# Where the vector engine norms the spatial gate's values: ahead of the next projection, or inside its first group of tiles

## The chip, the cores and the metric

The kernel runs on one core of one Trainium2 chip, as one program. The metric is device time in microseconds (us). Of the kernel before, three timed runs gave a median of 3325.25 us (3325.23 to 3325.48). Its traced execution took 3323.69 us, of which the trace spans 3322.0 us.

## The reference, cut to what matters

Two models run one after the other on 512 tokens of width 1024. The first has two layers, and only these are touched here. Each layer has a projection with eight parts (q, k, v, g, u, vs, p, gates), three branches (retention, spatial gating, pooling), and a feed-forward block of width 4096. Both halves of a layer are scaled and shifted by `mod`, which comes from the conditioning vector c:

```python
c_act = jax.nn.silu(c)
for l in range(DEPTH):                       # DEPTH = 2
    mod = c_act @ w_ada[l] + b_ada[l]        # 6 x 1024 numbers
    ...
    proj = h @ w_in[l]
    q, k, v, g, u, vs, p, gate_cols = split_columns(proj)
    y_ret = retention(q, k, v, g, positions)
    y_sgu = spatial_gating(u, vs, ws_gmlp[l], bs_gmlp[l], vnorm_gmlp[l])

def spatial_gating(u, v, w_s, b_s, v_gain):
    u = jax.nn.gelu(u)
    v = rms_norm(jax.nn.gelu(v), v_gain)     # over the 1024 channels of a token
    ...
    mixed = jnp.einsum('gts,bnsgc->bntgc', w, vc) + b_s.T[None, None, :, :, None]
    return u * mixed.reshape(B, S, GMLP_WIDTH)
```

The change concerns `v = rms_norm(gelu(v))`: its place among the work of the vector engine.

## The kernel before, in words

**Weights.** All weights come as one stream of 648 tiles of 128x1024 float32 (512 KB each), in the order in which they are used. A tile lands in one of four slots of `raw` (`RING = 4`). The scalar engine (ACT) makes the rounded part `hi[slot]` from it (line 1066), the vector engine (DVE) the rest `lo[slot] = raw - hi` (line 1514), and the tensor engine (PE) forms each product from three matmuls: hi by the high part of the data, hi by its low part, lo by its high part (lines 493 to 495). Both ACT and DVE have a helper `tick(s)` for this; it treats the slot that lies three ahead of the tile being worked on (`AHEAD = 3`). When DVE has made `lo`, it raises `lo_ready`; the sync engine waits for that before it issues the next load into the slot, and PE waits for it before it uses the tile.

**Conditioning sums.** Some of the stream's tiles are not for PE: they hold rows of `w_ada`. In three stages of a layer each group of four weight tiles comes with four such tiles. DVE multiplies one by `c_all` and sums it (`ada_sum`, line 1493) into a column of `four = stat[:, 0:4]`, and this too frees the slot (`lo_ready`). After four of them `take` copies `four` into `mod` (line 1500). The table `ADA_TICKS = ((0, 1), (2, 3, 4), (5, 6), (7,))` says which of the group's eight slots are treated beside tiles 0, 1, 2 and 3: numbers 0 to 3 are conditioning sums, 4 to 7 are weight tiles. ACT goes by the same table, but does nothing for 0 to 3.

**The order around the change.** Each engine runs its own list, in the order in which it is written. The stage before is the projection `vs` (`tiles_N(2, ...)`), token-major, whose four banks ACT drains with a Gelu into `act3` (line 1222). The stage after is the projection `u`, eight tiles (`tiles_T(8, ...)`), called u0 to u7 here, in two groups of four; ACT drains each with a Gelu (line 1216). Of a group, PE needs tile 3 from DVE's number 4 of that same group, and the tiles 0, 1 and 2 of the next group from its numbers 5, 6 and 7. So u4, the first tile of the second group, can begin when DVE has done number 5 of the first group, and the loads for u4 and what follows are issued when slots come free.

**The norm.** Between the two stages DVE waits until ACT has drained the last bank of `vs`, squares and sums each of the four token blocks (line 1822, four times), makes the mean plus epsilon (line 1825) and raises `v_mean`. ACT answers with a square root (line 1255) and raises `rooted`. DVE takes the reciprocal (1829), refines it with one Newton step (1831 to 1835), and scales the four blocks in place (1839). PE waits for the scaled blocks (`v_normed`) only after u7, in front of the mixing matmuls (line 736).

Lines of the loop helper (`repeat`, a hardware loop) show as line 83.

Of the kernel before, what the change touches and what calls it, by code (L numbers as in the profile page):

```python
# [10 lines left out]
ACT = mybir.ActivationFunctionType  # L11
ALU = mybir.AluOpType
# [4 lines left out]
D = 1024  # L17
KT = D // P
TT = S // P
# [5 lines left out]
EPS = 1e-6  # L25
# [67 lines left out]
def build(nc, stream, first, xT, cvec, pos, consts, decay, tables, vec1, ws, bs, vec2, wf, outT):  # L93
    with ExitStack() as ctx:
# [18 lines left out]
        yF = sb("yF", [P, 2 * KT * S])  # L113
        with nc.sbuf_tensor("halved", [P, 3 * KT, S], F32R) as halved:
            pass
        act3 = sb("act3", [P, 3 * KT, S])
# [18 lines left out]
        stat = sb("stat", [P, 16])  # L135
# [124 lines left out]
        bank_free = sem("bank_free")  # L260
# [24 lines left out]
        rooted = sem("rooted")  # L285
# [11 lines left out]
        v_mean = sem("v_mean")  # L297
        v_normed = sem("v_normed")
# [750 lines left out]
        def _(act):  # L1049
# [58 lines left out]
            def tiles_N(groups, drain, ada=False):  # L1108
                def body(i):
                    for s in range(2 * RING if ada else RING):  # L1110
                        tick(s, ada=ada and s < RING)
                    for t in range(TT):
                        token_wait(t)
                        drain(i, t)
                bodies(groups, {tok: 3, **(ada_ring if ada else {})}, body)
# [95 lines left out]
            for l in range(LAYERS):  # L1211
                round_h(mod[:, 0:8], tick_at=2)

                def drain_to(first, func):
                    def drain(i, s):
                        act.activation(act3[:, at(i * RING + s + first), :], pb[:, s:s + 1], func  # L1216
                                       ).then_inc(bank_free, 1)
                    return drain

                def drain_tok(first, func):  # L1220
                    def drain(i, t):
                        act.activation(act3[:, bass.ds(i + first + 2 * t, 1), :], pb[:, t:t + 1], func
                                       ).then_inc(bank_free, 1)
                    return drain
                tiles_T(8, lambda i, s: None, uses_st=False, peel=True)
                tiles_N(2, drain_tok(8, ACT.Copy))

                def head_out(h):

                    for e in range(2):  # L1230
                        o = pb[:, 2 + 2 * (h % 2) + e]
                        act.wait_ge(o_full, of.next())
                        act.activation(A[:, h + 4 * e], o, ACT.Copy)
                        act.activation(Osq[h % 2][:, e * S:(e + 1) * S], o, ACT.Square).then_inc(osq_ready, 1)

                def root_of(h):

                    act.wait_ge(summed, sums.next())
                    act.activation(stat[:, 8:12], pb[:, 0 if h < 2 else 6, 0:4], ACT.Sqrt, bias=epsc,
                                   scale=1.0 / R_V).then_inc(rooted, 1)  # L1240

                act.activation(cs[:, 2, 0:1], epsc, ACT.Sqrt)
                head_out(0)
                head_out(1)
                root_of(0)
                head_out(2)
                root_of(1)
                head_out(3)
                root_of(2)
                root_of(3)  # L1250
                tiles_T(8, lambda i, s: to_st(s, func=ACT.Silu))
                pairs(True)
                tiles_N(2, drain_tok(8, ACT.Gelu_apprx_tanh), ada=True)
                act.wait_ge(v_mean, means.next())
                act.activation(stat[:, 8:12], stat[:, 12:16], ACT.Sqrt).then_inc(rooted, 1)
                tiles_T(8, drain_to(0, ACT.Gelu_apprx_tanh), uses_st=False, ada=True)

                for n in range(KT):
                    s = n % RING
                    tick(s)  # L1260
                    act.wait_ge(tile_done, done.next())
                    act.wait_ge(y_ready, l * 56 + (8 + n + 1))
                    act.activation(A[:, n], pb[:, s], ACT.Copy).then_inc(bank_free, 1)
                pairs()
                for g in range(4):
                    tick(g)
                    act.wait_ge(tile_done, done.next())
                    for e in range(2):
                        n = 2 * g + e

                        to_st(n % 4, scale=v1[:, span(l * V_ALL + (V_PS + n), 1)], bias=bpps[:, n:n + 1])
                pairs(True)
                tick(0)
                to_x(peel=True)
                root()
                round_h(mod[:, 24:32])
                tiles_T(8, lambda i, s: to_st(s), peel=True)
                with repeat(act, 3, {split: 16, done: 16, stf: 8, **{c: 64 for c in land}}):
                    tiles_T(8, lambda i, s: None, uses_st=False)
                    tiles_T(8, lambda i, s: to_st(s))  # L1280
                if l < LAYERS - 1:
                    to_x()
                    root(then_tick=False)
                else:
                    act.wait_ge(gain_ready, 1)
                    late_tiles(to_late(hH, gain2, double=True))
# [179 lines left out]
            work = to_late(yH, v2[:, W_FFN + 8:W_FFN + 16])  # L1466
# [13 lines left out]
        def _(dve):  # L1480
            split, drained = Count(), Count(4)
# [15 lines left out]
            def take(i, m):  # L1497

                dve.drain()
                dve.tensor_copy(mod[:, bass.ds(i * RING + m, RING)], four)  # L1500
                dve.drain()
# [22 lines left out]
                    with repeat(dve, n, steps or ring) as i:  # L1524
                        body(i)

            def tiles_T(n, work, last=False, peel=False, ada=None, from_bank=False):
                def body(i, first=False):
                    for s in range(RING):
                        t = None if not last else TILES - RING * (n // RING - i) + s  # L1530
                        if ada is not None:
                            for j in ADA_TICKS[s]:
                                tick(j, ada=four[:, j:j + 1] if j < RING else None)
                            if s == 1:
                                take(i, ada)
                        elif s or not first:
                            tick(s, t)
                        done.next()
                        if work is None:
                            drained.next()  # L1540
                        elif from_bank:
                            drained.next()
                            dve.wait_ge(tile_done, done.value())
                            work(i, s)
                        else:
                            dve.wait_ge(bank_free, drained.next())
                            work(i, s)
                if peel:
                    body(0, True)
                    bodies(n // RING - 1, lambda i: body(i + 1))  # L1550
                    return
                bodies(n // RING, body, last, {**ring, **lands(2)} if ada is not None else None)
# [18 lines left out]
            roots = Count()  # L1571
# [177 lines left out]
            for l in range(LAYERS):  # L1749
# [66 lines left out]
                pairs(True, ada=16)  # L1816
                tiles_N(2, ada=32)

                dve.wait_ge(bank_free, drained.value())
                for t in range(TT):  # L1820
                    vt = act3[:, 8 + 2 * t:10 + 2 * t].rearrange("p a s -> p (a s)")
                    dve.tensor_tensor_reduce(yF[:, 0:1024], vt, vt, 1.0, 0.0, ALU.mult, ALU.add,
                                             stat[:, 8 + t:9 + t])
                    dve.drain()
                dve.tensor_scalar(stat[:, 12:16], stat[:, 8:12], 1.0 / D, EPS, ALU.mult, ALU.add)
                dve.drain().then_inc(v_mean, 1)
                y, v, t = stat[:, 8:12], stat[:, 12:16], stat[:, 4:8]
                dve.wait_ge(rooted, roots.next())
                dve.reciprocal(y, y)
                dve.drain()  # L1830
                dve.scalar_tensor_tensor(t, y, -0.5, y, ALU.mult, ALU.mult)
                dve.drain()
                dve.tensor_tensor(t, t, v, ALU.mult)
                dve.drain()
                dve.scalar_tensor_tensor(y, t, 1.5, y, ALU.add, ALU.mult)
                dve.drain()
                for t in range(TT):
                    vt = act3[:, 8 + 2 * t:10 + 2 * t].rearrange("p a s -> p (a s)")
                    dve.tensor_scalar(vt, vt, stat[:, 8 + t:9 + t], None, ALU.mult).then_inc(v_normed, 1)
                tiles_T(8, None, ada=40)  # L1840
                add_bias(l, 16, 48)
                dve.wait_ge(bank_free, drained.value())
                for n in range(KT):
# [473 lines left out]
```

## Time and profile before

| what | value |
|---|---|
| median of three timed runs | 3325.25 us (3325.23 to 3325.48) |
| profiled execution: own time | 3323.69 us |
| profiled execution: span of the trace | 3322.0 us |
| PE busy | 3273.8 us, 99% of the span |
| PE weight load busy (overlaps PE) | 2697.3 us, 81% |
| DVE busy | 1877.9 us, 57% |
| ACT busy | 1144.0 us, 34% |
| POOL busy | 146.6 us, 4% |
| chain that ended last | PE 90%, DVE 5%, the rest under 2% each |
| mean rate of the loads | 108 GB/s |

The own time includes 1.69 us that lie outside the trace's span. "Busy" counts the engine's instructions; a matmul of 512 columns shows as 0.39 us, though the next one starts 0.23 us later, since they overlap. In part 5 of the page a group's row ends in: busy us, mean ns of one | idle us before them, what ended most of it. So the pace of PE is read from the starts of its matmuls, not from their durations. A number in brackets behind a row is the time that the engine sat idle before it, and what ended that.

### The profile page before, as it was taken

The page shows a single profiled execution, that of the slowest core. Times are in us where ns is not written, and L with a number is a line of the kernel's source. Part 1 is how long each engine was busy: PE and PEld are TensorE (multiplying, and loading weights), DVE is VectorE, ACT ScalarE, POOL GpSimd, SP SyncE. Part 2 cuts the span into 40 slices and gives each one's busy share as a digit, 9 for nine tenths or more (in the row PEclk, how much of TensorE's full clock was granted, in tenths as well). Part 3 has the DMA queues.
Part 4 walks back from the last instruction along what each step waited for, and adds up shares of the span by engine and source line. Part 5 has one row for each costly group of instructions (what it writes and reads, how often), then busy time and mean ns, then how long its engine had stood idle before and what let it go on. Part 6 is the DMA issues. An engine that isn't in the chain of part 4 may idle for free.

```text
span 3322.0 us, 43128 instructions
## 1 busy us (share of the span) xinstructions
PE 3273.8 (99%) x15164; PEld 2697.3 (81%) x15164; DVE 1877.9 (57%) x2695; ACT 1144.0 (34%) x1494; POOL 146.6 (4%) x174
## 2 busy tenths in 40 slices
PE   7999999999999999999999999999999999999998
PEld 6788887888888788887888888768888887888887
DVE  6355557554446355557554445556665744576655
ACT  3333333332222233333332223364333513443333
POOL 1000000000000000000000002021000101010000
PEclk9999999999999999999999999999999999999999
DMA  6136424422222145324422222202222222112222
GB/s 232 70 127 210 145 89 146 158 89 95 95 101 83 64 142 200 140 88 160 150 89 95 95 101 87 83 20 89 102 101 96 102 102 83 45 69 101 97 95 76
DMA packets 98232, 357.79 MB, mean 108 GB/s; under 512 B 11104, under 2 KB 11120, under 8 KB 97856
## 3 DMA queue, kind: packets, MB, share of 16 engines
q1 hardware_dynamic: 97344, 353.73, 29.9%
q0 software_dynamic: 768, 2.47, 0.2%
q8 instruction: 75, 1.23, 0.1%
q14 instruction: 45, 0.37, 0.0%
HBM read 354.06 MB, written 2.10 MB: 107 GB/s over the span
## 4 chain that ended last, share of the span: by engine, by line
PE 90%; DVE 5%; issue 1%; ACT 1%; DMA 1%; DVEq 1%; SPq 0%; POOLq 0%; POOL 0%; ACTq 0%
PE pb L493 22%; PE pb L494 22%; PE pb L495 22%; PE pb L523 3%; PE pb L524 3%; PE pb L527 3%; PE pb L561 2%; PE pb L563 2%; PE pb L562 2%; DVE lo L1514 1%; PE pb L893 1%; PE pb L675 1%; DMA raw<-stream 1%; PE pb L998 1%; PE pb L847 1%
## 5 line engine op out<-in xcount | busy, mean ns | idle before, releaser
L1066 ACT ACTIVATE hi<-raw 128x1024 fp32r<-128x1024 f32 x549 | 577.4, 1056 | 995.6 <-PE pb L495 655.3
L1514 DVE TENSOR_TENSOR lo<-raw,hi 128x1024 fp32r<-128x1024 f32 (+1 forms) x549 | 671.6, 1228 | 369.8 <-ACT hi L1066 323.8
L493 PE MATMUL pb<-yH,hi 128*128 128x512 f32 x1648 | 641.6, 389 | 2.5 <-DVE lo L1514 2.5
L494 PE MATMUL pb<-yL,hi 128*128 128x512 f32 x1648 | 641.1, 389 | 0.0
L495 PE MATMUL pb<-yH,lo 128*128 128x512 f32 x1648 | 641.1, 389 | 0.0
L493 PE MATMUL pb<-hH,hi 128*128 128x512 f32 x1528 | 597.1, 391 | 4.3 <-DVE lo L1514 4.3
L495 PE MATMUL pb<-hH,lo 128*128 128x512 f32 x1528 | 594.6, 389 | 0.0
L494 PE MATMUL pb<-hL,hi 128*128 128x512 f32 x1528 | 594.6, 389 | 0.0
L493 PEld LDWEIGHTS pb<-yH,hi 128*128 128x128 f32 x1648 | 309.4, 188 | 67.7 <-ACT st L1079 3.3
L495 PEld LDWEIGHTS pb<-yH,lo 128*128 128x128 f32 x1648 | 309.4, 188 | 64.4
L494 PEld LDWEIGHTS pb<-yL,hi 128*128 128x128 f32 x1648 | 309.3, 188 | 64.0
L493 PEld LDWEIGHTS pb<-hH,hi 128*128 128x128 f32 x1528 | 286.9, 188 | 65.0 <-ACT act L1216 3.1
L495 PEld LDWEIGHTS pb<-hH,lo 128*128 128x128 f32 x1528 | 286.8, 188 | 59.8
L494 PEld LDWEIGHTS pb<-hL,hi 128*128 128x128 f32 x1528 | 287.0, 188 | 58.4
L1079 ACT ACTIVATE st<-pb 128x512 f32<-128x512 f32 x176 | 105.5, 599 | 508.9 <-PE pb L495 495.9
L1662 DVE SCALAR_TENSOR_TENSOR x<-pb,mod,x 128x512 f32 (+1 forms) x72 | 54.1, 751 | 192.8 <-PE pb L495 171.6
L493 PE MATMUL pb<-halved,hi 128*128 128x512 f32 x364 | 142.1, 390 | 2.2 <-DVE lo L1514 1.3
L495 PE MATMUL pb<-halved,lo 128*128 128x512 f32 x364 | 141.6, 389 | 0.0
L494 PE MATMUL pb<-halved,hi 128*128 128x512 f32 x364 | 141.6, 389 | 0.0
L1493 DVE CUSTOM_DVE_ANT_0 raw<-raw,pb 128x1024 f32<-128x1024 f32 x96 | 112.5, 1218 | 39.0 <-ACT st L1079 24.1
L1956 DVE TENSOR_TENSOR st<-pb,tab 128x512 f32<-128x512 f32 x88 | 60.9, 692 | 89.8 <-PE pb L495 66.8
L402 POOL TENSOR_TENSOR act<-act 128x512 f32<-128x512 f32 x25 | 33.8, 1352 | 1699.6 <-ACT act L1120 1699.0
(341 smaller groups left out, 3873.4 us busy)
## 6 DMA issues: line engine op xcount, KB each, us to landing
raw<-stream SPq DMA_DIRECT2D x648, 512.0 KB, 3.2
yF<-first SPq DMA_DIRECT2D x8, 512.0 KB, 12.9
act<-first SPq DMA_DIRECT2D x8, 512.0 KB, 17.5
x<-xT SPq DMA_DIRECT2D x1, 2048.0 KB, 9.3
outT<-act SPq DMA_DIRECT2D x8, 256.0 KB, 2.2
tab<-decay SPq DMA_DIRECT2D x1, 1024.0 KB, 6.5
scr<-ws POOLq DMA_DIRECT2D x2, 256.0 KB, 4.3
scr<-bs POOLq DMA_DIRECT2D x2, 256.0 KB, 5.4
```

The source lines that it names most:

```text
L493: pe.matmul(out, whi, ahi, start=first, stop=False)
L494: pe.matmul(out, whi, alo, start=False, stop=False)
L495: return pe.matmul(out, wlo, ahi, start=False, stop=last)
L523: pe.matmul(pb[:, s], hi[:, s, w], aH[:, k], start=k == 0, stop=False)
L524: pe.matmul(pb[:, s], lo[:, s, w], aH[:, k], start=False, stop=False)
L527: ins = pe.matmul(pb[:, s], hi[:, s, w], aL[:, k], start=False, stop=k == ks - 1)
L561: pe.matmul(pb[:, t], aH[:, k, a], hi[:, s, w], start=k == 0, stop=False)
L562: pe.matmul(pb[:, t], aL[:, k, a], hi[:, s, w], start=False, stop=False)
L1066: act.activation(hi[:, s], raw[:, s], ACT.Copy).then_inc(hi_ready, 1)
L1079: act.activation(st[:, s:s + 1], pb[:, b:b + 1], func, bias=bias, scale=scale).then_inc(bank_free, 1)
L1493: dve.tensor_tensor_reduce(w, w, c_all, 1.0, 0.0, ALU.mult, ALU.add, m).then_inc(lo_ready, 1)
L1514: dve.tensor_tensor(lo[:, s, 0:width], raw[:, s, 0:width], hi[:, s, 0:width].bitcast(F32), ALU.subtract).then_inc(lo_ready, 1)
```

## The change

DVE no longer does the norm ahead of the stage `u`, but within its first group of four tiles: behind conditioning sums 0 to 3, the weight tile number 4 and `take`, ahead of the weight tiles 5, 6 and 7. For this the call of eight tiles becomes two calls of four on DVE and on ACT, and DVE's `tiles_T` gets an argument `between` with a function that runs in the group's second step. On ACT the square root moves from ahead of the eight drains to between the first four and the last four. The wait for the drained banks of `vs` goes with the norm. PE, POOL and the sync engine keep their lists.

```diff
@@ ACT
                 tiles_N(2, drain_tok(8, ACT.Gelu_apprx_tanh), ada=True)
+                tiles_T(4, drain_to(0, ACT.Gelu_apprx_tanh), uses_st=False, ada=True)
                 act.wait_ge(v_mean, means.next())
                 act.activation(stat[:, 8:12], stat[:, 12:16], ACT.Sqrt).then_inc(rooted, 1)
-                tiles_T(8, drain_to(0, ACT.Gelu_apprx_tanh), uses_st=False, ada=True)
+                tiles_T(4, drain_to(4, ACT.Gelu_apprx_tanh), uses_st=False, ada=True)
@@ DVE, the helper
-            def tiles_T(n, work, last=False, peel=False, ada=None, from_bank=False):
+            def tiles_T(n, work, last=False, peel=False, ada=None, from_bank=False, between={}):
 ...
                             if s == 1:
                                 take(i, ada)
+                            if s in between:
+                                between[s]()
@@ DVE, the stage
                 tiles_N(2, ada=32)
 
-                dve.wait_ge(bank_free, drained.value())
-                for t in range(TT):
+                def v_norm():
+
+                    for t in range(TT):
 ...
-                tiles_T(8, None, ada=40)
+                v_drained = drained.value()
+                tiles_T(4, None, ada=40, between={1: lambda: (dve.wait_ge(bank_free, v_drained), v_norm())})
+                tiles_T(4, None, ada=44)
```

The body of `v_norm` is the norm's code as it was, from the sums of squares to the scaling.

DVE's list of instructions from the end of the stage `vs` on, before. `yF` takes the squares, `stat` the small statistics, `act` are the values of `vs`, and `lo<-raw,hi` is a weight tile of line 1514:

```order
L1500 COPY mod<-stat 128x4
...
L1822 ISA yF,stat<-act 128x1024 [waits bank_free]
...
L1829 RECIPROCAL stat<-stat 128x4 [waits rooted]
...
L1839 TENSOR_SCALAR act<-act,stat 128x1024 x4
...
L1493 ISA raw,stat<-raw,pb 128x1024 [waits landed3]
...
L1514 TENSOR_TENSOR lo<-raw,hi 128x1024 [waits hi_ready]
```

The same stretch of DVE's list with the change (its lines stand one to seven further down in the file):

```order
L1501 COPY mod<-stat 128x4
...
L1494 ISA raw,stat<-raw,pb 128x1024 [waits landed3]
...
L1515 TENSOR_TENSOR lo<-raw,hi 128x1024 [waits hi_ready]
L1501 COPY mod<-stat 128x4
L1826 ISA yF,stat<-act 128x1024 [waits bank_free]
...
L1833 RECIPROCAL stat<-stat 128x4 [waits rooted]
...
L1843 TENSOR_SCALAR act<-act,stat 128x1024 x4
L1515 TENSOR_TENSOR lo<-raw,hi 128x1024 [waits hi_ready] x3
```

The four sums and the first weight tile have moved ahead of the norm; the three other weight tiles of the group stand behind it, and so behind its wait for `rooted`.

ACT's list at the same place, before. `stat<-stat` is the square root, `act<-pb` drains a tile of `u`, `hi<-raw` is the rounded part of a weight tile:

```order
L1255 ACT_TABLE_LOAD
L1255 ACTIVATE stat<-stat 128x4 [waits v_mean]
...
L1216 ISA [waits tile_done]
L1216 ACT_TABLE_LOAD
L1216 ACTIVATE act<-pb 128x512
...
L1066 ACTIVATE hi<-raw 128x1024 [waits tile_done]
```

And with the change:

```order
L1216 ACTIVATE act<-pb 128x512 [waits tile_done]
L1066 ACTIVATE hi<-raw 128x1024 [waits tile_done,landed3]
L1216 ACTIVATE act<-pb 128x512 [waits tile_done]
L1066 ACTIVATE hi<-raw 128x1024 [waits tile_done,landed0]
L1066 ACTIVATE hi<-raw 128x1024 [waits tile_done,landed1]
L1216 ACTIVATE act<-pb 128x512 [waits tile_done]
L1066 ACTIVATE hi<-raw 128x1024 [waits tile_done,landed2]
L1216 ACTIVATE act<-pb 128x512 [waits tile_done]
...
L1256 ACT_TABLE_LOAD
L1256 ACTIVATE stat<-stat 128x4 [waits v_mean]
```

The square root has moved behind the drains of u0, u1, u2 and u3, each of which waits until PE has finished that tile.

## Rows read from the trace of the kernel before

**Rows 1.** Page, parts 4 and 5: chain by engine; the costliest ACT group.
```profile
PE 90%; DVE 5%; issue 1%; ACT 1%; DMA 1%; DVEq 1%; SPq 0%; POOLq 0%; POOL 0%; ACTq 0%
L1066 ACT ACTIVATE hi<-raw 128x1024 fp32r<-128x1024 f32 x549 | 577.4, 1056 | 995.6 <-PE pb L495 655.3
```

**Rows 2.** Waits of PE: who was waited for, total us, times, longest us.
```profile
PE pb L493 <- DVE lo L1514: 8.1, 8, 1.3
```

**Rows 3.** Timeline of PE, first layer: start us, us, instruction [idle before].
```profile
344.24 0.39 PE L493 MATMUL pb<-hH,hi 128*128 128x512 f32 x1
...
360.33 0.39 PE L495 MATMUL pb<-hH,lo 128*128 128x512 f32 x1
361.76 0.49 PE L493 MATMUL pb<-hH,hi 128*128 128x512 f32 x1 [1.05 <-DVE lo L1514]
...
367.10 0.39 PE L495 MATMUL pb<-hH,lo 128*128 128x512 f32 x1
367.33 0.39 PE L493 MATMUL pb<-hH,hi 128*128 128x512 f32 x1
```

**Rows 4.** Timeline of PE, second layer, the same place.
```profile
1352.26 0.39 PE L495 MATMUL pb<-hH,lo 128*128 128x512 f32 x1
1353.90 0.49 PE L493 MATMUL pb<-hH,hi 128*128 128x512 f32 x1 [1.25 <-DVE lo L1514]
...
1359.45 0.39 PE L493 MATMUL pb<-hH,hi 128*128 128x512 f32 x1
```

**Rows 5.** Timeline of DVE, first layer, around the norm.
```profile
345.17 1.22 DVE L1822 CUSTOM_DVE_ANT_0 yF<-act 128x1024 f32<-128x1024 f32 x1 [3.49 <-ACT act L1222]
...
350.99 0.18 DVE L1829 RECIPROCAL stat<-stat 128x4 f32<-128x4 f32 x1 [0.30 <-ACT stat L1255]
...
351.95 2.74 DVE L1839 TENSOR_SCALAR act<-act,stat 128x1024 f32<-128x1024 f32 x4
354.61 1.22 DVE L1493 CUSTOM_DVE_ANT_0 raw<-raw,pb 128x1024 f32<-128x1024 f32 x1
...
360.41 1.23 DVE L1514 TENSOR_TENSOR lo<-raw,hi 128x1024 fp32r<-128x1024 f32 x1 [1.15 <-ACT hi L1066]
```

**Rows 6.** Timeline of ACT, first layer, around the square root.
```profile
344.53 0.60 ACT L1222 ACTIVATE act<-pb 128x512 f32 x1 [0.76 <-PE pb L563]
345.15 1.28 ACT L1255 ACT_TABLE_LOAD   x1
350.75 0.21 ACT L1255 ACTIVATE stat<-stat 128x4 f32<-128x4 f32 x1 [4.31 <-DVEq L1826]
350.98 1.28 ACT L1216 ACT_TABLE_LOAD   x1
352.28 0.60 ACT L1216 ACTIVATE act<-pb 128x512 f32 x1
...
367.63 0.60 ACT L1216 ACTIVATE act<-pb 128x512 f32 x1 [1.86 <-PE pb L495]
```

**Rows 7.** The line that issues the loads, 340 to 390 us: landing.
```profile
DMA to landing us min/median/max: 3.1/4.3/5.3
```

**Rows 8.** Timeline of PE after idle times of 3.91 and 2.52 us.
```profile
43.73 0.79 PE L523 MATMUL pb<-hH,hi 128*128 128x512 f32 x1 [3.91 <-ACT hH L1183]
...
45.18 0.63 PE L524 MATMUL pb<-hH,lo 128*128 128x512 f32 x1
45.61 0.63 PE L523 MATMUL pb<-hH,hi 128*128 128x512 f32 x1
...
47.59 0.39 PE L523 MATMUL pb<-hH,hi 128*128 128x512 f32 x1
...
2947.17 0.47 PE L523 MATMUL pb<-yH,hi 128*128 128x512 f32 x1 [2.52 <-DVE x L2173]
2947.47 0.40 PE L524 MATMUL pb<-yH,lo 128*128 128x512 f32 x1
```

**Rows 9.** Windows: us, busy of PE, PEld, DVE, ACT, POOL, PEclk, DMA share, GB/s.
```profile
2030.50:2033.90 3.40, 3.40 (x10) 2.60 (x9) 1.08 (x7) 0.00 (x0) 0.00 (x0) 0.51 0.03 7
```

More of the change, by code:

```diff
@@ L1817, in _ @@
                 tiles_N(2, ada=32)
-                dve.wait_ge(bank_free, drained.value())
-                for t in range(TT):
-                    vt = act3[:, 8 + 2 * t:10 + 2 * t].rearrange("p a s -> p (a s)")
-                    dve.tensor_tensor_reduce(yF[:, 0:1024], vt, vt, 1.0, 0.0, ALU.mult, ALU.add,
-                                             stat[:, 8 + t:9 + t])
-                    dve.drain()
-                dve.tensor_scalar(stat[:, 12:16], stat[:, 8:12], 1.0 / D, EPS, ALU.mult, ALU.add)
@@ L1826, in _ @@
[L1826 to L1839, printed above, removed]
-                tiles_T(8, None, ada=40)
+                def v_norm():
+                    for t in range(TT):
+                        vt = act3[:, 8 + 2 * t:10 + 2 * t].rearrange("p a s -> p (a s)")
+                        dve.tensor_tensor_reduce(yF[:, 0:1024], vt, vt, 1.0, 0.0, ALU.mult, ALU.add,
+                                                 stat[:, 8 + t:9 + t])
+                        dve.drain()
+                    dve.tensor_scalar(stat[:, 12:16], stat[:, 8:12], 1.0 / D, EPS, ALU.mult, ALU.add)
+                    dve.drain().then_inc(v_mean, 1)
+                    y, v, t = stat[:, 8:12], stat[:, 12:16], stat[:, 4:8]
+                    dve.wait_ge(rooted, roots.next())
+                    dve.reciprocal(y, y)
+                    dve.drain()
+                    dve.scalar_tensor_tensor(t, y, -0.5, y, ALU.mult, ALU.mult)
+                    dve.drain()
+                    dve.tensor_tensor(t, t, v, ALU.mult)
+                    dve.drain()
+                    dve.scalar_tensor_tensor(y, t, 1.5, y, ALU.add, ALU.mult)
+                    dve.drain()
+                    for t in range(TT):
+                        vt = act3[:, 8 + 2 * t:10 + 2 * t].rearrange("p a s -> p (a s)")
+                        dve.tensor_scalar(vt, vt, stat[:, 8 + t:9 + t], None, ALU.mult).then_inc(v_normed, 1)
```

## The prediction

> **What bounds the kernel.** I read the page first, then the waits of PE, then the timelines of PE, DVE and ACT about the place of the change, in both layers. The chain that ended last is PE for 90% and DVE for 5% [rows 1]: a change on DVE or ACT counts only by the time for which it makes PE wait. The waits of PE hold one kind that fits here: PE's weight tile not ready, because DVE had not made its `lo` part, eight times, 8.1 us in all [rows 2]. The timeline of PE shows two of these at the changed place. In the first layer 72 matmuls (u0, u1, u2) run from 344.24 at 0.2266 us each (71 steps up to 360.33), so u3 could begin at 360.56; it begins at 361.76 [rows 3]. That is 1.20 us lost. In the second layer it is 1353.90 against 1352.49, so 1.41 us [rows 4]. The reason is in DVE's timeline: it waits 3.49 us for the last drain of `vs`, norms from 345.17 to 354.61, and only then frees slots by its sums, so u3's weights land late and their `lo` starts at 360.41 [rows 5].
>
> So the most that this place can give back is 1.20 + 1.41 = 2.6 us, 0.08% of the run.
>
> **What the change does, step by step.** No arithmetic is added or taken away: what moves is the norm of one layer's values (four squares with sums, the mean, the Newton step, four scalings on DVE; the square root and its table load on ACT), once in each of the two layers. The two engines' lists of the first four tiles decide the rest.
>
> *The sums and u3's weights.* DVE had nothing to do for the 3.49 us ahead of 345.17 [rows 5], so its four sums (1.22 us each) start near 341.7 and free slots some 13 us earlier than before (354.61). A load lands at most 5.3 us after its issue [rows 7]. The rounded part of u3's weights stands on ACT behind the drain of u0. u0's last matmul starts at 344.24 + 23 x 0.2266 = 349.45; a drain starts 0.53 us after the last matmul of its tile (367.10 to 367.63) [rows 3, 6], so at 349.98, takes 0.60, and `hi` takes 1.06 [rows 1]. `lo` is made by about 352.9, and PE wants u3 at 360.56. The old stall goes, with more than 7 us to spare.
>
> *The norm up to its mean.* It begins near 353.4, and takes what it took, 5.5 us from 345.17 up to the reciprocal's wait (350.69) [rows 5]. `v_mean` is up at about 359. An error of several us here changes nothing, as the next step shows.
>
> *The square root.* This is the step that decides. On ACT it now stands behind the drains of u0 to u3, and the last of them waits for PE to finish u3. DVE meanwhile stands at the reciprocal, which waits for `rooted`, and behind this on DVE stand weight tiles 5, 6 and 7 of the group, the first of which is u4's `lo`. PE can't begin u4 without it. So PE finishes u3, and only then starts a chain that it has to wait for in full:
> - u3 begins at 360.56 (no stall now), its last matmul at 360.56 + 5.21 = 365.77, PE is out of work at 366.00;
> - ACT drains u3 from 366.30 (0.53 later, as above);
> - the load of the root's table starts 0.62 later (344.53 to 345.15), at 366.92 [rows 6];
> - the root starts 1.30 after its table load, by the pair 350.98 and 352.28 [rows 6], at 368.22;
> - the reciprocal starts 0.24 after the root (350.75 to 350.99) [rows 5, 6], at 368.46;
> - reciprocal and Newton step take 0.96 up to 351.95, the four scalings 2.66 more up to 354.61 [rows 5]: 372.08;
> - `lo` of u4 starts there, and PE starts 1.35 after a `lo` started (360.41 to 361.76) [rows 3, 5]: 373.43.
>
> PE idles from 366.00 to 373.43, 7.4 us. Before, u4 began at 367.33 [rows 3]: 6.10 us lost in the first layer. In the second layer u0 began at 1352.49 - 16.32 = 1336.17, so u4 will begin 29.19 later, at 1365.36, against 1359.45 [rows 4]: 5.91 us. Together 12.0 us. The 2.6 us of the old stalls are already counted in this as gained.
>
> The Trainium skill ("ScalarE: Activation LUTs", What ACT_TABLE_LOAD costs) puts a switch of tables at about 2.66 us, a load of 1.28 and a drain behind it. The trace has 1.28 for the load and 1.30 from its start to the next activation [rows 6], so here nothing shows behind it. By the page each chain would be 1.36 us longer.
>
> *The clock of PE.* An idle time as long as 7.4 us is nowhere in the stretches shown, so it is bounded from both sides. After 3.91 us idle (at the start of the program) the matmuls came at 0.43 us a step from 43.73 to 47.59, instead of 0.23: nine matmuls in 3.86 us which else take 2.04, so 1.8 us lost [rows 8]. In a stretch near 2030 us the granted clock was 0.51 for 3.4 us, which is the level of 1.2 GHz and costs 1.7 us [rows 9]. After 2.52 us idle the pace was full, 1.2 GHz did not show [rows 8]: 0 us. An idle time of 7.4 us is past the longer of the two, so I take 1.8 us a layer, and 3.6 for both. The lower end is 0; the upper is a low clock twice as long as seen, 3.6 a layer, 7.2 for both. A gain from idling is excluded, since the pace is full before. The Trainium skill ("TensorE: Matmul & The Clock Gate", Why this matters for your kernels) also has idle gaps between matmul bursts bring the low clock back; the row after 3.91 us agrees.
>
> *What comes behind.* The second group starts on DVE with its `lo` tiles at 372.1 and 1.23 us each, then its sums: the first sum is done near 377, and it issues the load of u7's weights, landed by 382.3 at the latest [rows 7]. The last of the four sums waits for the slot freed near 375.8, landed by 381.1. `hi` and `lo` of u7 are done by about 385.5; PE wants u7 at 373.43 + 3 x 5.44 = 389.8. So no second stall, with 4 us of cover. `v_normed` is up at 372.1, and PE asks for it behind u7, over 20 us later. The loads of the mixing stage are later by less than PE is. All of the rest shifts as a whole, and nothing there waits for a fixed time, so nothing is given back.
>
> **The sum.** 6.1 + 5.9 + 3.6 = 15.6 us. On the profiled execution's own time that is 3323.69 + 15.6 = 3339.3. The median of the runs is 1.56 above this execution, so for the median 3325.25 + 15.6 = 3340.9 us, slower by 0.47%.
>
> **Rivals.**
>
> *The stall without the low clock.* For it: the 2.52 us idle that left no trace. Against it: 3.91 us that did. It gives 3325.25 + 12.0 = 3337.3. 10%.
>
> *No stall at all, so not slower.* The place is the wait for `rooted`. PE is not held if the reciprocal starts by 366.00 - 1.35 - 2.66 - 0.96 = 361.03. The mean is up at 359, so this holds if ACT takes the square root between two drains, at 361 or before. Then the chain hides, the old stalls go, and the time is 3325.25 - 2.6 = 3322.6, within the bound of 0.2%. Against it: each engine runs its list in order, and in ACT's list the root stands behind u3's drain, which can't start before 366.30. 3%.
>
> *The change has no effect worth seeing.* Stall out, stall in, of about the same size: it needs the chain behind u3 to be some 6 us shorter than its pieces, that is a step missing, such as the table load and the four scalings (1.30 and 2.66) off the path. Nothing in the lists lets them off. About 3325, 2%.
>
> *The table switch costs what the page says.* The root never followed its table load directly in the trace (345.15, then 350.75 [rows 6]), so the pair that I used belongs to the Gelu. If the root waits longer behind the load, by as much as the load itself again (1.28), each layer loses 1.3 more: 3343.5. 4%. By the page's own 1.36 it would be 3343.6.
>
> *The second group starves too.* The cover of 4 us is used up only if a load lands 9 us after its issue, against 5.3 at most. Each us beyond costs 1 us a layer; with one, 3342.9. 3%.
>
> **Chances and range.** The forecast holds the remaining 78%, with a range of its own of 3338.5 to 3344.5 (clock costs 1 to 7.2 us, half a us either way on the chains). For 8 in 10 with room for the case without the low clock: 3336.5 to 3345.0. A difference under 0.2% (6.7 us) is about what a measurement of this kernel can't tell from no change. Faster by over that: 1%, since even the best case gives 2.6 us. Within it: 5%, the two cases without a net stall. Slower: 94%.
>
> **What would show it.** In PE's timeline of the changed kernel, no idle time ahead of u3, and about 7.4 us idle ahead of the matmul that begins u4, once in each layer, released by DVE's `lo`. On DVE about 9 us idle ahead of the reciprocal, released by ACT's square root. On ACT the root about 2 us behind the drain of u3's bank. Matmuls at 0.43 us a step for 3 to 4 us from u4's start, and a granted clock under 1 there. Sums of the first group from near 342. I am wrong if the reciprocal starts before ACT drained u3, if PE idles under 5 us, or if the second group shows idle time of PE again.

## The result and the profile after

The changed kernel took 3340.69 us (median of six runs, 3338.76 to 3341.45), the kernel before 3325.24 us beside it (six runs, 3322.98 to 3327.50). The ratio is 1.0047, with a 95% interval of 1.0037 to 1.0058: slower by 0.47%. The forecast was 3340.9 us, with a range of 3336.5 to 3345.0. In a second session the changed kernel took 3340.35 us against 3325.04, ratio 1.0046 (1.0032 to 1.0060).

The profiled execution after took 3341.19 us with a span of 3339.5, against 3323.69 and 3322.0: 17.5 us more.

Page of the changed kernel, part 4 (chain by engine) and the first row of its waits of PE (us in total, times, longest us), which answer to [rows 1, 2]:

```profile
PE 91%; DVE 4%; issue 1%; DMA 1%; ACT 1%; DVEq 1%; SPq 0%; POOLq 0%; POOL 0%; ACTq 0%
```

```profile
PE pb L493 <- DVE lo L1515: 19.9, 8, 7.2
```

Eight waits as before, but 19.9 us in place of 8.1, and the longest 7.2 in place of 1.3. Timeline of PE, first layer, against [rows 3]:

```profile
344.94 0.39 PE L493 MATMUL pb<-hH,hi 128*128 128x512 f32 x1
...
361.25 0.39 PE L493 MATMUL pb<-hH,hi 128*128 128x512 f32 x1
...
366.47 0.39 PE L495 MATMUL pb<-hH,lo 128*128 128x512 f32 x1
374.02 0.79 PE L493 MATMUL pb<-hH,hi 128*128 128x512 f32 x1 [7.16 <-DVE lo L1515]
374.60 0.63 PE L494 MATMUL pb<-hL,hi 128*128 128x512 f32 x1
375.03 0.63 PE L495 MATMUL pb<-hH,lo 128*128 128x512 f32 x1
...
379.30 0.63 PE L493 MATMUL pb<-hH,hi 128*128 128x512 f32 x1
379.72 0.53 PE L494 MATMUL pb<-hL,hi 128*128 128x512 f32 x1
380.09 0.40 PE L495 MATMUL pb<-hH,lo 128*128 128x512 f32 x1
```

u0 begins at 344.94, 0.70 us later than before for reasons that lie ahead of the change. u3 begins at 361.25, 72 steps of 0.2266 behind it: the old idle time is gone. PE is out of work at 366.70 and begins u4 at 374.02, 7.3 us later; then it steps at 0.43 us until 380. The second layer, against [rows 4]:

```profile
1366.02 0.39 PE L495 MATMUL pb<-hH,lo 128*128 128x512 f32 x1
1373.57 0.79 PE L493 MATMUL pb<-hH,hi 128*128 128x512 f32 x1 [7.17 <-DVE lo L1515]
...
1376.30 0.58 PE L493 MATMUL pb<-hH,hi 128*128 128x512 f32 x1
1376.71 0.40 PE L494 MATMUL pb<-hL,hi 128*128 128x512 f32 x1
```

Timeline of DVE in the changed kernel, first layer, against [rows 5]:

```profile
342.72 1.22 DVE L1494 CUSTOM_DVE_ANT_0 raw<-raw,pb 128x1024 f32<-128x1024 f32 x1 [0.35 <-issue]
...
352.15 1.23 DVE L1515 TENSOR_TENSOR lo<-raw,hi 128x1024 fp32r<-128x1024 f32 x1 [4.78 <-ACT hi L1066]
353.47 0.17 DVE L1501 COPY mod<-stat 128x4 f32<-128x4 f32 x1
353.76 1.23 DVE L1826 CUSTOM_DVE_ANT_0 yF<-act 128x1024 f32<-128x1024 f32 x1
...
359.11 0.17 DVE L1829 TENSOR_SCALAR stat<-stat 128x4 f32<-128x4 f32 x1
369.04 0.18 DVE L1833 RECIPROCAL stat<-stat 128x4 f32<-128x4 f32 x1 [9.76 <-ACT stat L1256]
...
370.01 2.74 DVE L1843 TENSOR_SCALAR act<-act,stat 128x1024 f32<-128x1024 f32 x4
372.66 3.49 DVE L1515 TENSOR_TENSOR lo<-raw,hi 128x1024 fp32r<-128x1024 f32 x3
```

The mean is done at 359.28, and DVE then stands still for 9.76 us. Timeline of ACT, against [rows 6]:

```profile
361.45 0.60 ACT L1216 ACTIVATE act<-pb 128x512 f32<-128x512 f32 x1 [2.95 <-PE pb L495]
...
366.89 0.60 ACT L1216 ACTIVATE act<-pb 128x512 f32<-128x512 f32 x1 [3.89 <-PE pb L495]
367.51 1.28 ACT L1256 ACT_TABLE_LOAD   x1
368.80 0.21 ACT L1256 ACTIVATE stat<-stat 128x4 f32<-128x4 f32 x1
```

u3's drain at 366.89, the table load behind it, the root at 368.80, the reciprocal at 369.04: the chain of the prediction. ACT itself was idle for 3.89 us ahead of that drain, with the mean long there; it stood in its list at a drain whose tile PE had not finished.

Windows of the changed kernel (us, busy of PE, PEld, DVE, ACT, POOL, PEclk, DMA share, GB/s), against [rows 9]:

```profile
369.40:373.40 4.00, 0.00 (x0) 0.00 (x0) 3.77 (x8) 0.91 (x1) 0.00 (x0) 0.54 0.00 0
373.40:377.00 3.60, 2.98 (x7) 2.41 (x8) 3.60 (x4) 0.00 (x0) 0.00 (x0) 0.50 0.44 162
```

The granted clock falls to its lower level, 1.2 GHz, while PE still waits, and is there when u4 begins.

### The profile page after: what moved, and what is told of

It is laid out like the page before. It is cut to its first block, busy times and chain, and to the rows that moved or that the text cites. A ratio compares the mean times of both kernels' runs of the same rounds, so it can differ in the third digit from the quotient of the medians.

```text
span 3339.5 us, 43062 instructions
## 1 busy us (share of the span) xinstructions
PE 3279.7 (98%) x15164; PEld 2701.8 (81%) x15164; DVE 1878.0 (56%) x2695; ACT 1141.5 (34%) x1492; POOL 146.6 (4%) x174
## 4 chain that ended last, share of the span: by engine, by line
PE 91%; DVE 4%; issue 1%; DMA 1%; ACT 1%; DVEq 1%; SPq 0%; POOLq 0%; POOL 0%; ACTq 0%
PE pb L493 23%; PE pb L494 23%; PE pb L495 23%; PE pb L523 3%; PE pb L524 3%; PE pb L527 3%; PE pb L561 2%; PE pb L562 2%; PE pb L563 2%; DVE lo L1515 1%; PE pb L893 1%; PE pb L675 1%; DMA raw<-stream 1%; PE pb L985 1%; PE pb L998 1%
## 5 line engine op out<-in xcount | busy, mean ns | idle before, releaser
L493 PE MATMUL pb<-hH,hi 128*128 128x512 f32 x1528 | 599.1, 392 | 16.3 <-DVE lo L1515 16.3
```

The source lines that it names most:

```text
L493: pe.matmul(out, whi, ahi, start=first, stop=False)
```

## The experiments

All are timed against the kernel before beside them, and each stands as edits of the changed kernel unless said otherwise.

### The root somewhere else on ACT

`e1_root_before_u2`: the square root and its wait go behind the `hi` parts of tiles 5 and 6.

```diff
+                            if s in between:
+                                between[s]()
...
-                tiles_T(4, drain_to(0, ACT.Gelu_apprx_tanh), uses_st=False, ada=True)
-                act.wait_ge(v_mean, means.next())
-                act.activation(stat[:, 8:12], stat[:, 12:16], ACT.Sqrt).then_inc(rooted, 1)
+                def v_root():
+
+                    act.wait_ge(v_mean, means.next())
+                    act.activation(stat[:, 8:12], stat[:, 12:16], ACT.Sqrt).then_inc(rooted, 1)
+
+                tiles_T(4, drain_to(0, ACT.Gelu_apprx_tanh), uses_st=False, ada=True, between={2: v_root})
```

(The first two lines stand in ACT's `tiles_T`, behind the weight tiles of step `s`.)

> The changed kernel, but ACT takes the square root behind the hi parts of tiles 5 and 6 and ahead of its wait for u2, in place of behind u3's drain. DVE's list is that of the changed kernel. Theory (the root stands behind u3's drain, DVE waits there, and u4's lo stands behind the wait): in the changed kernel the mean is up at 359.3 and ACT is free from 358.5, so the root comes near 360, the reciprocal right after, u4's lo near 364, some 2 us before PE wants it. No idle time of PE ahead of u3 or u4, no low clock: 2.6 us under the kernel before, near 3322.6 (ratio 0.999). Rival (DVE's order alone costs, the norm in the group is simply too much work there): PE idles several us ahead of u4, 3330 or more. Rival (the extra switch of ACT's tables between drains holds the hi parts or the banks): an idle time of some 1 to 3 us later in the group.

Measured: 3321.33 us (11 runs) against 3325.10, ratio 0.9990 (0.9981 to 0.9999). PE's waits for `lo` are six in all, and none stands in this stage. Timelines of ACT and DVE of this kernel, first layer:

```profile
357.90 1.28 ACT L1259 ACT_TABLE_LOAD   x1
359.20 0.20 ACT L1259 ACTIVATE stat<-stat 128x4 f32<-128x4 f32 x1
359.42 1.28 ACT L1218 ACT_TABLE_LOAD   x1
360.83 0.60 ACT L1218 ACTIVATE act<-pb 128x512 f32<-128x512 f32 x1
```

```profile
359.43 0.18 DVE L1838 RECIPROCAL stat<-stat 128x4 f32<-128x4 f32 x1 [0.78 <-ACT stat L1259]
...
363.06 3.49 DVE L1520 TENSOR_TENSOR lo<-raw,hi 128x1024 fp32r<-128x1024 f32 x3
```

DVE waits 0.78 us for the root in place of 9.76, and u4's `lo` starts at 363.06, in time. DVE's list is the same as in the changed kernel. So the place of one instruction on ACT carries the whole loss: 3340.7 against 3321.3. The rival that DVE's order alone costs is out, and so is the one of the added table switch.

### The norm somewhere else on DVE

`e3_norm_between_groups`: ACT's list is that of the changed kernel; on DVE the norm goes behind tiles 5, 6 and 7.

```diff
-                tiles_T(4, None, ada=40, between={1: lambda: (dve.wait_ge(bank_free, v_drained), v_norm())})
+                tiles_T(4, None, ada=40)
+                dve.wait_ge(bank_free, v_drained)
+                v_norm()
                 tiles_T(4, None, ada=44)
```

> The changed kernel, but DVE does the whole norm between the two groups of four tiles, behind weight tiles 5, 6 and 7 of the first. ACT's list is that of the changed kernel, so the root still stands behind u3's drain, and DVE still waits for it. Theory (what costs is that u4's lo stands behind that wait, not the wait itself): DVE waits as long, up to about 368.4 us, but PE has u4, u5 and u6 ready. u7's weights are freed late, near 373, lo by about 380, PE wants them at 382. No idle time of PE: near 3322.6 (ratio 0.999). Rival (DVE's 9 us of waiting cost in any place): 3337 or more. Rival (u7 now comes late): an idle time of up to 3 us ahead of u7, about 3325 to 3330.

Measured: 3322.33 us (11 runs), ratio 0.9991 (0.9982 to 1.0000). No idle time of PE in this stage. But one part of the expectation missed. Timeline of DVE:

```profile
361.88 1.23 DVE L1515 TENSOR_TENSOR lo<-raw,hi 128x1024 fp32r<-128x1024 f32 x1 [3.08 <-ACT hi L1066]
363.02 1.22 DVE L1826 CUSTOM_DVE_ANT_0 yF<-act 128x1024 f32<-128x1024 f32 x1
...
368.83 0.18 DVE L1833 RECIPROCAL stat<-stat 128x4 f32<-128x4 f32 x1 [0.30 <-ACT stat L1256]
```

I had DVE wait long for the root here too. It does not: tile 7's `hi` comes at 361.88 only, so the squares start at 363.02 and the mean is later than u3's drain; ACT waits for DVE. What the run shows is still the point: the root comes even later than in the changed kernel, 3.1 us behind the end of u3 (368.59 and 365.54) against 2.1, and with u4's `lo` ahead of the wait for it, PE loses nothing. That a wait of 9 us on DVE would cost nothing in this place is not shown, since here DVE waits for 0.30 us only.

`e7_norm_before_tile4`: only the four sums go ahead of the norm, and the root is where it was before, ahead of all drains.

```diff
-                tiles_T(4, drain_to(0, ACT.Gelu_apprx_tanh), uses_st=False, ada=True)
                 act.wait_ge(v_mean, means.next())
                 act.activation(stat[:, 8:12], stat[:, 12:16], ACT.Sqrt).then_inc(rooted, 1)
+                tiles_T(4, drain_to(0, ACT.Gelu_apprx_tanh), uses_st=False, ada=True)
...
-                tiles_T(4, None, ada=40, between={1: lambda: (dve.wait_ge(bank_free, v_drained), v_norm())})
+                tiles_T(4, None, ada=40, between={4: lambda: (dve.wait_ge(bank_free, v_drained), v_norm())})
```

(`between` is asked here with the number of the tile, ahead of its `tick`.)

> DVE does the four conditioning sums first, then the norm, then weight tiles 4 to 7; ACT takes the square root ahead of all drains of u, as in the kernel before. This moves the sums alone ahead of the norm. Theory (the sums free the slots; the root is the only other thing that matters): norm from 347 to about 356.5, u3's lo near 358, 2.6 us before PE wants it at 360.6; no idle time ahead of u3 or u4: near 3322.6 (ratio 0.999). Rival (the old idle time ahead of u3 came from ACT, which drains u0 late because of the root): u3 still 1 us late, 3325.

Measured: 3322.49 us (11 runs), ratio 0.9993 (0.9984 to 1.0002), which alone can't be told from no change. The trace can: u3's `lo` starts at 355.87 and no idle time of PE is left at u3 or u4. So the old idle time came from the sums standing behind the norm, and not from ACT, where the root still stands ahead of all drains.

`e2_split_only`: the kernel before, with its call of eight tiles cut in two on both engines.

```diff
-                tiles_T(8, drain_to(0, ACT.Gelu_apprx_tanh), uses_st=False, ada=True)
+                tiles_T(4, drain_to(0, ACT.Gelu_apprx_tanh), uses_st=False, ada=True)
+                tiles_T(4, drain_to(4, ACT.Gelu_apprx_tanh), uses_st=False, ada=True)
...
-                tiles_T(8, None, ada=40)
+                tiles_T(4, None, ada=40)
+                tiles_T(4, None, ada=44)
```

> The kernel before, with the call of eight tiles cut into two calls of four on DVE and ACT, and the norm and the root where they were. Theory: cutting costs nothing, 3325.2 and the old idle times of 1.2 and 1.4 us ahead of u3 stay (ratio 1.000). Rival (loop entry and exit, or other code, costs time on ACT or DVE): idle time of PE ahead of u4 too, some tenths to 2 us a layer.

Measured: 3325.03 us (11 runs), ratio 1.0002 (0.9993 to 1.0011). The old waits stand where they stood (timeline of PE, both layers), and there are no others in the stage:

```profile
361.62 0.49 PE L493 MATMUL pb<-hH,hi 128*128 128x512 f32 x1 [1.08 <-DVE lo L1515]
...
1353.81 0.49 PE L493 MATMUL pb<-hH,hi 128*128 128x512 f32 x1 [1.24 <-DVE lo L1515]
```

### The sizes of the terms

`e5_scale_late`: the four scalings leave the chain.

```diff
+                def v_scale():
+
                     for t in range(TT):
                         vt = act3[:, 8 + 2 * t:10 + 2 * t].rearrange("p a s -> p (a s)")
                         dve.tensor_scalar(vt, vt, stat[:, 8 + t:9 + t], None, ALU.mult).then_inc(v_normed, 1)
...
                 tiles_T(4, None, ada=40, between={1: lambda: (dve.wait_ge(bank_free, v_drained), v_norm())})
+                v_scale()
                 tiles_T(4, None, ada=44)
```

> The changed kernel, but the four scalings of the norm stand between the two groups of tiles, behind weight tiles 5, 6 and 7; squares, mean, root and Newton step stay inside the first group. Theory (every step between u3's drain and u4's lo is on the path at its full length): u4 begins 2.66 us earlier in each layer, PE idles 4.7 us in place of 7.3. The low clock may stay (4.7 us is past the 3.9 after which it was seen): 3340.7 - 5.3 = 3335.4, less if the low clock gets shorter, down to 3331.5 if it goes. Rival (other work hides behind the scalings): less than 2 us gained in all.

Measured: 3335.16 us (6 runs), ratio 1.0032 (1.0020 to 1.0044). Timeline of PE, first layer:

```profile
365.65 0.39 PE L495 MATMUL pb<-hH,lo 128*128 128x512 f32 x1
370.56 0.79 PE L493 MATMUL pb<-hH,hi 128*128 128x512 f32 x1 [4.52 <-DVE lo L1515]
```

From the end of u3 (365.88) to u4 it is 4.68 us, 2.64 less than the 7.32 of the changed kernel: the scalings (2.65 from 370.01 to 372.66 there) were on the path at their full length.

`e6_no_gelu_u`: a root of a constant ahead of the drains loads the table; the drains of u are copies, so the Gelu of u is left out.

```diff
+                act.activation(cs[:, 2, 0:1], epsc, ACT.Sqrt)
-                tiles_T(4, drain_to(0, ACT.Gelu_apprx_tanh), uses_st=False, ada=True)
+                tiles_T(4, drain_to(0, ACT.Copy), uses_st=False, ada=True)
                 act.wait_ge(v_mean, means.next())
                 act.activation(stat[:, 8:12], stat[:, 12:16], ACT.Sqrt).then_inc(rooted, 1)
-                tiles_T(4, drain_to(4, ACT.Gelu_apprx_tanh), uses_st=False, ada=True)
+                tiles_T(4, drain_to(4, ACT.Copy), uses_st=False, ada=True)
```

> The changed kernel, with the eight tiles of u drained by a plain copy; the Gelu of u is left out. So ACT can load the root's table ahead of the drains, and the root follows u3's drain without a load. Theory (the table load of 1.28 us is on the path): PE idles 6.0 us in place of 7.3 ahead of u4, 2.6 us less in all, 3338 with the low clock as it was. Rival (a page of the notes has 1.38 us more behind each switch of tables): 2.7 us a layer less, 3335. Rival (the load is hidden): no difference, 3340.7.

Measured: 3337.97 us (5 runs), ratio 1.0040 (1.0026 to 1.0054). Timelines of ACT and of PE, first layer:

```profile
366.37 0.60 ACT L1216 ACTIVATE act<-pb 128x512 f32<-128x512 f32 x1 [3.89 <-PE pb L495]
366.87 0.20 ACT L1257 ACTIVATE stat<-stat 128x4 f32<-128x4 f32 x1
```

```profile
365.95 0.39 PE L495 MATMUL pb<-hH,lo 128*128 128x512 f32 x1
372.08 0.79 PE L493 MATMUL pb<-hH,hi 128*128 128x512 f32 x1 [5.74 <-DVE lo L1516]
```

From the drain's start to the root it is 0.50 us, against 1.91 in the changed kernel, and PE waits 5.90 us, 1.42 less. So the table load was on the path, and it costs what the trace shows of it, 1.3 us, with a tenth more. The larger price of the Trainium skill ("ScalarE: Activation LUTs", What ACT_TABLE_LOAD costs), 2.66 us for a switch, would have taken 1.2 us more off each wait; this run does not bear it out.

`e4_busy_pe`: PE is kept at work between u3 and u4.

```diff
-                tiles_T(8, hH, hL, None, ada=True)
+                tiles_T(4, hH, hL, None, ada=True)
+                for _ in range(30):
+                    pe.matmul(pb[:, 5], hH[:, 0, 0:P], hH[:, 0], start=True, stop=True)
+                tiles_T(4, hH, hL, None, ada=True)
```

> The changed kernel, with 30 matmuls of 512 columns into an unused bank between u3 and u4 on PE (their product is used by nothing), 6.8 us at full pace, so that PE works through its 7.3 us of waiting. Theory (behind the wait PE runs at 1.2 GHz for a while, and this is 2.8 us in the first layer and 1.3 in the second of the trace of the changed kernel): no matmul at 0.43 us a step behind u4's start, u4 begins when it did, and the time falls by about 4 us against the changed kernel, to 3337. Rival (the low clock costs nothing that counts, since DVE and the loads would set the pace of the second group anyway): the time stays at 3340.7.

Measured: 3337.52 us (5 runs), ratio 1.0038 (1.0024 to 1.0051), beside 3340.35 for `after_again`. Timeline of PE, first layer, and windows (columns as above):

```profile
365.45 6.96 PE L729 MATMUL pb<-hH 128*128 128x512 f32 x30
372.70 0.50 PE L493 MATMUL pb<-hH,hi 128*128 128x512 f32 x1 [0.29 <-DVE lo L1518]
373.04 0.40 PE L494 MATMUL pb<-hL,hi 128*128 128x512 f32 x1
373.27 0.39 PE L495 MATMUL pb<-hH,lo 128*128 128x512 f32 x1
```

```profile
365.50:372.50 7.00, 6.91 (x31) 5.39 (x29) 4.40 (x9) 3.37 (x4) 0.00 (x0) 1.00 0.00 0
372.50:378.00 5.50, 5.30 (x23) 4.42 (x24) 4.77 (x7) 0.00 (x0) 0.00 (x0) 1.00 0.67 210
```

u4 begins 7.25 us behind the end of u3, as late as in the changed kernel, but at 0.23 us a step. The medians differ by 2.8 us where 4 were expected; with runs that spread over 3 us that is no contradiction. The slowest of the five runs (3338.24) is under the fastest of `after_again` (3338.65), so the low clock costs time.

`after_again`, the changed kernel beside these:

> The changed kernel once more, beside the others on one chip. Theory: 15 us over the kernel before, 3340.7, with a spread of 1 to 3 us between runs as the low clock behind each wait comes out shorter or longer.

Measured: 3340.35 us (5 runs, 3338.65 to 3341.71).

## Why the prediction was right

**The bound.** PE sets the time, and DVE and ACT count only through its waits. All runs agree: each median is that of the kernel before plus what PE's timeline shows in this stage, waits and low clock, to within 1.2 us (`e1_root_before_u2` is furthest off: 3.8 us gained where the two idle times hold 2.6).

**The sums and u3.** Right: sums from 342.72, the norm from 353.76 (forecast: near 353.4, on a program that starts 0.7 us earlier), no wait ahead of u3. `e7_norm_before_tile4` shows that this part alone takes both old idle times away, the 2.6 us.

**The chain behind u3.** Forecast 7.43 us from the end of u3 to u4, measured 7.32 in both layers; the difference is the drain of u3, which starts 0.42 us after the last matmul (366.47 to 366.89) and not 0.53. Counted from u0's start, u4 begins at 29.08 in place of 29.19. Before, it was 23.09 and 23.28 (1359.45 - 1336.17), so the loss is 5.99 and 5.80 us, 11.8 in all against 12.0. The experiments took two links out, and each gave back its length: 2.64 for the scalings, 1.42 for the table load.

**The low clock.** The mechanism was right, the size somewhat low. In the first layer 14 steps took 6.07 us (374.02 to 380.09) which at full pace take 3.17, so 2.9 lost; in the second, seven steps took 3.14 (1373.57 to 1376.71) for 1.59, so 1.6 lost. Together 4.5 us against 3.6, inside the bounds of 0 and 7.2.

Those bounds rested on thin rows. In the kernel before, PE went on at full pace behind 2.52 us of idle time [rows 8]; the prediction took that for "0 us". At the same place of the changed kernel, where the lists of the engines are the same, the idle time is again 2.52 us, and a few matmuls later PE steps at 0.43 us (timeline of PE, changed kernel):

```profile
2963.05 0.47 PE L523 MATMUL pb<-yH,hi 128*128 128x512 f32 x1 [2.52 <-DVE x L2180]
...
2964.61 0.63 PE L523 MATMUL pb<-yH,hi 128*128 128x512 f32 x1
2965.03 0.63 PE L524 MATMUL pb<-yH,lo 128*128 128x512 f32 x1
```

Of the ten traces of this case, six have a stretch at 0.43 us a step there (`after`, `after_again`, `e2_split_only`, `e4_busy_pe`, `e6_no_gelu_u`, `e7_norm_before_tile4`) and four have none (`before`, `e1_root_before_u2`, `e3_norm_between_groups`, `e5_scale_late`). So whether a low clock follows such a wait differs from one execution to the next, and one trace that shows none is no proof of 0. The other row used as a price, near 2030 us [rows 9], follows no long wait at all: ahead of it PE ran sixteen matmuls of one column (from 2027.23) and then some of 512 columns at full pace. The longer waits of this stage had the low clock behind them every time (4.7, 5.9 and 7.3 us, in four traces, both layers).

**What comes behind.** No later wait in the second group, as forecast. The loads took longer to land than I had as their upper bound: 6.2 us at most in this stretch (3.1/4.6/6.2), against 5.3. The cover held all the same: u7's `lo` starts at 384.18, and PE takes u7 at 393.28.

**The sum against the trace.** 11.8 + 4.5 = 16.3 us, and the spans differ by 17.5. Of the rest 0.7 was there at u0. Between the two layers 1.3 us come back, and in the second layer's end they go again; both in the norm sums of the feed-forward block, where twelve small matmuls take 2.91 us in one execution and 1.58 in another. Timelines of PE, before and after, first layer:

```profile
675.79 2.91 PE L571 MATMUL pb<-cst 128*128 128x128 f32 x12
```

```profile
685.33 1.58 PE L571 MATMUL pb<-cst 128*128 128x128 f32 x12
```

In the second layer the changed kernel has the 2.91 (at 1683.88) and the kernel before the 1.58 (at 1668.07). The longer ones are stretches of low clock too: the granted clock is at its lower level from about 675 to 679 us in the one trace and from about 1684 to 1688 in the other. `e2_split_only`, which has the old order, shows such a stretch in both places, so I put none of this down to the change. The last 0.5 us are spread over the rest of the program. These stretches, which come and go between executions, and the length of the low clock behind each wait are of the size by which runs of one kernel differ, 1 to 3 us. The mean clock of a run does not sort the runs, though: of the changed kernel's, three with 0.989 took 3341.2 to 3341.5 and one with 0.995 took 3338.8, but a run of `after_again` with 0.990 took 3338.65.

**Luck.** That the forecast of 3340.9 lies 0.2 us from the median of 3340.69 is partly luck. The chains came out 0.2 us shorter than forecast and the low clock of the profiled execution 0.9 us dearer, and the medians differ by 15.45 us where that trace adds up to 16.3. What is not luck is the wait: its place, its cause and each link of its length. One sum of the prediction does not come out: chains of 12.0 us, half a us either way, and a clock cost of 1 to 7.2 give 3337.8 to 3345.0, and not its own range of 3338.5 to 3344.5; the measured time lies in both.

Not tried: a root on ACT behind u2's drain, which by the same sum would leave a wait of some 2 us (an estimate).

## What to carry to other kernels

When work that needs an answer from a second engine is moved, look up where the answer stands in the other engine's list, and what that engine waits for ahead of it. Here a gap of 1.2 us was traded for one of 7.3 us since the answer stood behind a drain that waits for PE, while PE's next tile stood behind the question. The sound forms of the same idea put the answer where that engine is free (`e1_root_before_u2`, and `e7_norm_before_tile4`, where the root stands ahead of all drains), or the next tile ahead of the question (`e3_norm_between_groups`); they measured 3321.3 to 3322.5 us, about 0.1% below the kernel before. For two of them the interval reaches to no change (1.0000 and 1.0002); that PE's idle times are gone from the timeline is the surer sign.

## What the runs showed of the hardware

The low clock behind the same idle time of 7.3 us lasted for 14 matmuls of 512 columns in one layer and 7 in the other (13 and 7 in `after_again`), so the price of one such wait is 1.5 to 2.9 us on top of the wait. Behind 4.7 us of idle time (`e5_scale_late`) it was there as well: ten slow steps in 4.41 us from 370.56, 2.1 us lost, and 1.7 in the second layer. Behind 2.5 us (between 2944 and 2964 us of the program) it came in six of ten traces. Thirty matmuls without a use, put into the wait, kept the clock at its full level through 7 us.
